# RWKV head groups: the elementwise preparation of the next group is queued beside the block inverse of the current one, behind the scan of the group before; five working buffers get memory of their own

## The reference, cut to what matters

```python
    w = -jax.nn.softplus(-(w0 + jnp.tanh(wl) @ w2)) - 0.5
    a = jax.nn.sigmoid(a0 + al @ a2)
    g = jax.nn.sigmoid(gl) @ g2
    kk = heads(k * k_k)
    kk = kk * lax.rsqrt(jnp.sum(kk * kk, axis=-1, keepdims=True) + 1e-12)
    k = k * (1.0 + (a - 1.0) * k_a)
    decay = jnp.exp(-jnp.exp(heads(w)))

    def step(state, inp):
        r_t, k_t, v_t, kk_t, b_t, d_t = inp
        sa = jnp.einsum('bhvk,bhk->bhv', state, -kk_t)
        state = (state * d_t[:, :, None, :] + sa[..., None] * b_t[:, :, None, :]
                 + v_t[..., None] * k_t[:, :, None, :])
        return state, jnp.einsum('bhvk,bhk->bhv', state, r_t)
...
    y = ((y - mean) * lax.rsqrt(var + LNX_EPS)).reshape(bsz, s, RWKV_W)
    y = y * lnx_g.astype(jnp.float32) + lnx_b.astype(jnp.float32)
    y = y + bonus.reshape(bsz, s, RWKV_W)
    return (y * g.astype(jnp.float32)).astype(feat.dtype)
```

## Time and profile before

| | us |
|---|---|
| median of 3 runs (2466.19 to 2469.96) | 2467.66 |
| time of the profiled execution | 2463.41 |
| its span | 2461.6 |
| PE busy | 2324.6 (94%) |
| DVE busy | 1233.2 (50%) |
| RWKV section, first preparation to last group | 265.6 to 531.0 |

### The profile page before, as it was taken

The page is one execution under the profiler, slowest core; times in us unless marked ns, Lnnn a source line. Parts: engine busy times, 40 slices in busy tenths (PEclk is TensorE's granted clock), DMA queues, the critical chain, the costliest instruction groups (busy, mean ns, idle before and its releaser), DMA issues.

```text
span 2461.6 us, 30787 instructions
## 1 busy us (share of the span) xinstructions
PE 2324.6 (94%) x12524; PEld 1654.6 (67%) x12524; DVE 1233.2 (50%) x2169; ACT 746.1 (30%) x1172; POOL 646.4 (26%) x288
## 2 busy tenths in 40 slices
PE   8989787797999989999999999999999999999999
PEld 3334455544444467668878888888766887888887
DVE  4455555533556531774355767310187445577610
ACT  3333222212111143443233333223354223333311
POOL 0000000002000033224444444444313444444443
PEclk9999888878999999999999999999999999999999
DMA  5521000035999932113333333222211333333322
GB/s 220 135 71 35 15 2 2 2 134 196 373 409 409 356 114 88 60 52 95 94 94 95 98 99 94 93 96 98 86 52 61 94 95 93 96 101 94 95 80 99
DMA packets 80258, 287.79 MB, mean 117 GB/s; under 512 B 9299, under 2 KB 10323, under 8 KB 79478
## 3 DMA queue, kind: packets, MB, share of 16 engines
q1 hardware_dynamic: 76726, 279.56, 33.1%
q0 software_dynamic: 1408, 4.20, 0.5%
q10 hardware_dynamic: 1984, 2.06, 0.2%
HBM read 278.11 MB, written 16.07 MB: 120 GB/s over the span
## 4 chain that ended last, share of the span: by engine, by line
PE 80%; DVE 9%; DMA 5%; issue 3%; ACT 2%; POOL 1%; ACTq 0%; SPq 0%; DVEq 0%; another core or an unknown queue 0%; POOLq 0%
PE bank L1899 12%; PE bank L1901 12%; PE bank L1900 12%; PE bank L529 5%; DMA arena<-in_stream 4%; PE bank L2048 3%; PE bank L2049 3%; PE bank L2047 3%; DVE arena L392 3%; PE bank L1513 2%; PE bank L855 2%; PE bank L1884 2%; PE bank L1886 2%; PE bank L1885 2%; PE bank L1481 2%
## 5 line engine op out<-in xcount | busy, mean ns | idle before, releaser
L1634 POOL TENSOR_TENSOR ring_low<-ring,W_high 128x1024 fp32r<-128x1024 f32 x252 | 606.2, 2406 | 1124.5 <-ACT W_high L402 1124.5
L1899 PE MATMUL bank<-H_high,W_high 128*128 128x512 f32 x1408 | 555.5, 395 | 7.9 <-ACT arena L402 5.9
L1901 PE MATMUL bank<-H_high,ring_low 128*128 128x512 f32 x1408 | 548.5, 390 | 0.0
L1900 PE MATMUL bank<-H_low,W_high 128*128 128x512 f32 x1408 | 548.1, 389 | 0.0
L402 ACT ACTIVATE W_high<-ring 128x1024 fp32r<-128x1024 f32 x264 | 279.8, 1060 | 872.2 <-PE bank L1901 552.6
L1899 PEld LDWEIGHTS bank<-H_high,W_high 128*128 128x128 f32 x1408 | 264.3, 188 | 77.9 <-issue 23.2
L1901 PEld LDWEIGHTS bank<-H_high,ring_low 128*128 128x128 f32 x1408 | 264.3, 188 | 55.9
L1900 PEld LDWEIGHTS bank<-H_low,W_high 128*128 128x128 f32 x1408 | 264.4, 188 | 55.7 <-issue 1.9
L392 DVE TENSOR_TENSOR arena<-bank,root 128x512 f32<-128x512 f32 x116 | 79.7, 688 | 309.9 <-PE bank L1901 309.7
L402 ACT ACTIVATE arena<-bank 128x512 f32<-128x512 f32 (+5 forms) x175 | 74.6, 438 | 315.2 <-PE bank L830 115.9
L398 DVE SCALAR_TENSOR_TENSOR arena<-arena 128x512 f32<-128x512 f32 (+3 forms) x63 | 117.8, 1870 | 99.1 <-ACT arena L406 98.5
(11 more groups left out here) (264 smaller groups left out, 3239.2 us busy)
## 6 DMA issues: line engine op xcount, KB each, us to landing
ring<-in_stream SPq DMA_DIRECT2D x289, 512.0 KB, 3.6
arena<-in_stream SPq DMA_DIRECT2D x31, 2048.0 KB, 12.9
arena<-in_stream SPq DMA_DIRECT2D x31, 1024.0 KB, 10.2
sorted_x<-in_zero_row SPq DMA_DIRECT2D x4, 2048.0 KB
arena<-sorted_x SPq DMA_DIRECT2D x15, 512.0 KB, 16.3
X<-in_x SPq DMA_DIRECT2D x2, 1024.0 KB, 7.9
ring<-in_stream SPq DMA_DIRECT2D x1, 2048.0 KB, 7.9
out<-X SPq DMA_DIRECT2D x8, 256.0 KB, 7.0
```

What stands on the lines that cost most here:

```text
L1634: return G.tensor_tensor(ring_low[:, slot, :], ring[:, slot, :], W_high[:, s % 2, :].bitcast(F32), ALU.subtract)
L1899: mm(ps[:, :], wh[:, k, :], H_high[:, k, :], start=k == 0, stop=False)
L1900: mm(ps[:, :], wh[:, k, :], H_low[:, k, :], start=False, stop=False)
L1901: i = mm(ps[:, :], wl[:, k, :], H_high[:, k, :], start=False, stop=k == KD - 1)
```

## The change: what it does

The generator has three streams now. `rwkv_early` holds the elementwise preparation, cut into `feed` (ru, ra, the two tanh), `rows` (DVE only), `roots` (rkk and ACT's exponentials), `root` (DVE only), `bonus` and `turned`. `rwkv_invert` holds blocks, keyed, the levels and read. `rwkv_scan` is as it was. In round c the inverse of group c, the scan of group c-1 and the early part of group c+1 are dealt out: "i", "s" and "e". Round 0 has no scan and round 3 no early part. The scan of group 3 stands alone at the end, as before. Step and state stand next to each other, between two parts of the inverse.

The product rg and the transpose of v, with their two ACT copies, move from the start of the preparation to its end. The halves get places of their own: half 0 after `feed` of group 0, half 1 after its `roots`, half 2 after its `bonus`, 3 and 4 after `feed` and `bonus` of group 1, 5 after `bonus` of group 2, 6 and 7 after `feed` and `bonus` of group 3. DVE's addition stands at the same place in DVE's queue. Before, there were two halves in each group.

Five buffers of the inverse (MT, TT, TKA, XX, MK) shared memory with buffers of the preparation (LW, A, KK, SQ, RS). They lie in `early` now, over uq, uk and uv, and DVE's wait for `read` of the group before falls away.

```diff
-def rwkv_prepare(c):
-
-    for part in ("rows", "root", "bonus", "turned", "blocks", "keyed"):
-        yield part, c, 0
+def rwkv_invert(c):
+
+    yield "blocks", c, 0
+    yield "keyed", c, 0
     for lev in LEVELS:
         yield "cross", c, lev
         yield "grow", c, lev
...
-BESIDE = "pss" * 4 + "ps" * 10 + "pspp"
+def rwkv_early(c):
+
+    for part in ("feed", "rows", "roots", "root", "bonus", "turned"):
+        yield part, c, 0
+
+
+HALVES_AT = {("feed", 0): [0], ("roots", 0): [1], ("bonus", 0): [2], ("feed", 1): [3], ("bonus", 1): [4], ("bonus", 2): [5], ("feed", 3): [6], ("bonus", 3): [7]}
+BESIDE = "iss" * 4 + "e" + "iss" + "e" + "iss" * 2 + "e" + "iss" + "is" + "e" + "is" * 2 + "e" + "ii" + "e"
...
 def rwkv_order():
 
-    yield from rwkv_prepare(0)
-    for c in range(3):
-        prepare, scan = rwkv_prepare(c + 1), rwkv_scan(c)
+    def with_halves(part):
+        yield part
+        for m in HALVES_AT.get(part[:2], []):
+            yield "half", 0, m
+
+    for part in rwkv_early(0):
+        yield from with_halves(part)
+    for c in range(4):
+        invert, scan, early = rwkv_invert(c), rwkv_scan(c - 1) if c else iter(()), rwkv_early(c + 1) if c < 3 else iter(())
         for who in BESIDE:
-            yield next(prepare if who == "p" else scan)
-        yield from prepare
-        yield from scan
+            part = next({"i": invert, "s": scan}.get(who, early), None)
+            if part is not None:
+                yield from with_halves(part)
+        for rest in (scan, invert, early):
+            assert next(rest, None) is None
     yield from rwkv_scan(3)
...
-    return {"rows": [f"ru{c}", f"ra{c}", f"rg{c}", f"wp{2 * c}", f"rt{c}_v"], "root": [f"rkk{c}"], "bonus": [f"rb{c}", f"wp{2 * c + 1}"],
-            "turned": [f"rt{c}_{x}" for x in "bka"], "blocks": [f"m{x}{c}_{hh}" for x in PRODUCTS for hh in range(2)],
+    return {"feed": [f"ru{c}", f"ra{c}"], "rows": [], "roots": [f"rkk{c}"], "root": [], "bonus": [f"rb{c}"], "half": [f"wp{n}"],
+            "turned": [f"rt{c}_{x}" for x in "bkav"] + [f"rg{c}"], "blocks": [f"m{x}{c}_{hh}" for x in PRODUCTS for hh in range(2)],
...
-        W.update(YB=W["LW"], MT=W["LW"], TT=W["A"], TKA=W["KK"], KH=W["KK"], KT=W["KP"], BT=W["B"], XX=W["SQ"], MK=W["RS"],
+        W.update(YB=W["LW"], KH=W["KK"], KT=W["KP"], BT=W["B"],
                  BH=W["ENL"], AT=W["ELX"])
+        for i, n in enumerate(("MT", "TT", "TKA", "XX", "MK")):
+            W[n] = par(w1, W1, "uq", 512 * i, 512)
...
-            if part == "rows":
+            if part == "half":
+                latent_half(pe, n, range(4))
+            elif part == "feed":
...
+            elif part == "roots":
+                pe.e.wait_ge(*pe.emptied(f"rkk{c}"))
+                pe.e.wait_ge(*pe.nth("kksq", c + 1))
...
+            elif part == "bonus":
+                pe.e.wait_ge(*pe.emptied(f"rb{c}"))
+                pe.e.wait_ge(*pe.nth("rkr", c + 1))
...
+            elif part == "turned":
+                pe.e.wait_ge(*pe.nth("hats", c + 1))
+                for x, src in (("b", W["BH"]), ("k", W["KH"]), ("a", W["AT"]), ("v", RAW[:, 8 + c, 1:513])):
+                    turn_feature(pe, c, x, src)
                 pe.e.wait_ge(*pe.emptied(f"rg{c}"))
...
                 mm(bank_of(f"rg{c}")[:, :], par(w1, W1, "g2", c * P, P), RAW[:, 13, 1:513], start=True, stop=True).then_inc(pe.fills(f"rg{c}"), 1)
-                latent_half(pe, 2 * c, range(0, 2))
-                turn_feature(pe, c, "v", RAW[:, 8 + c, 1:513])
-            elif part == "root":
-                pe.e.wait_ge(*pe.emptied(f"rkk{c}"))
-                pe.e.wait_ge(*pe.nth("kksq", c + 1))
-                mm(bank_of(f"rkk{c}")[:, :], cc("blk64"), W["SQ"], start=True, stop=True).then_inc(pe.fills(f"rkk{c}"), 1)
-                latent_half(pe, 2 * c, range(2, 4))
...
-                latent_half(pe, 2 * c + 1, range(4))
-            elif part == "turned":
-                pe.e.wait_ge(*pe.nth("hats", c + 1))
-                for x, src in (("b", W["BH"]), ("k", W["KH"]), ("a", W["AT"])):
...
-            if part == "rows":
+            if part == "feed":
...
-                sc.e.wait_ge(*sc.filled(f"rg{c}"))
-                if c >= 2:
-                    sc.e.wait_ge(*sc.nth("rw_out", c - 1))
-                act_(W[f"G{q}"], bank_of(f"rg{c}")[:, :], ACT.Copy).then_inc(sc.takes(f"rg{c}"), 1)
-                sc.e.wait_ge(*sc.filled(f"rt{c}_v"))
-                act_(W[f"TKV{q}"], bank_of(f"rt{c}_v")[:, :], ACT.Copy).then_inc(sc.takes(f"rt{c}_v"), 1)
-            elif part == "root":
+            elif part == "roots":
                 log_exp_tables()
...
             elif part == "turned":
-                for x, d in (("b", f"TKB{q}"), ("k", f"TKK{q}"), ("a", "TKA")):
+                for x, d in (("b", f"TKB{q}"), ("k", f"TKK{q}"), ("a", "TKA"), ("v", f"TKV{q}")):
                     sc.e.wait_ge(*sc.filled(f"rt{c}_{x}"))
                     act_(W[d], bank_of(f"rt{c}_{x}")[:, :], ACT.Copy).then_inc(sc.takes(f"rt{c}_{x}"), 1)
+                sc.e.wait_ge(*sc.filled(f"rg{c}"))
+                if c >= 2:
+                    sc.e.wait_ge(*sc.nth("rw_out", c - 1))
+                act_(W[f"G{q}"], bank_of(f"rg{c}")[:, :], ACT.Copy).then_inc(sc.takes(f"rg{c}"), 1)
...
-            if part == "rows":
-                if c:
-                    dv.e.wait_ge(*dv.filled(f"rta{c - 1}_1"))
+            if part == "half":
+                add_latent_half(dv, n)
+            elif part == "feed":
                 ts(w["KK"], k_, one("k_k"), None, ALU.mult).then_inc(dv.tells("kk0"), 1)
+            elif part == "rows":
...
                 tt(c64(w["KH"]), c64(w["KT"]), dc, ALU.mult).then_inc(dv.tells("hats"), 1)
                 V.tensor_copy(w[f"DC{q}"], c64(w["EL"])[:, :, 63]).then_inc(dv.chained(), 1)
-                add_latent_half(dv, 2 * c)
             elif part == "bonus":
                 dv.e.wait_ge(*dv.filled(f"rb{c}"))
                 tt(w[f"BON{q}"], bank_of(f"rb{c}")[:, :], v_, ALU.mult).then_inc(dv.takes(f"rb{c}"), 1)
-                add_latent_half(dv, 2 * c + 1)
```

More of the change, by code:

```diff
@@ L458, in build @@
             W[f"DC{q}"] = arena[:, 27968 + 8 * q:27976 + 8 * q]
-        W.update(YB=W["LW"], MT=W["LW"], TT=W["A"], TKA=W["KK"], KH=W["KK"], KT=W["KP"], BT=W["B"], XX=W["SQ"], MK=W["RS"],
+        W.update(YB=W["LW"], KH=W["KK"], KT=W["KP"], BT=W["B"],
                  BH=W["ENL"], AT=W["ELX"])
+        for i, n in enumerate(("MT", "TT", "TKA", "XX", "MK")):
+            W[n] = par(w1, W1, "uq", 512 * i, 512)
+        assert [W1[n] for n in ("uq", "uk", "uv")] == [(0, 1536), (1536, 512), (2048, 512)]
         halves_ = [slice(0, 64), slice(64, 128)]
@@ L719, in rwkv_pe @@
                 mm(bank_of(f"ra{c}")[:, :], w2a2[64:128, cw], RAW[64:128, 12, 1:513], start=True, stop=True).then_inc(pe.fills(f"ra{c}"), 1)
+            elif part == "roots":
+                pe.e.wait_ge(*pe.emptied(f"rkk{c}"))
+                pe.e.wait_ge(*pe.nth("kksq", c + 1))
+                mm(bank_of(f"rkk{c}")[:, :], cc("blk64"), W["SQ"], start=True, stop=True).then_inc(pe.fills(f"rkk{c}"), 1)
+            elif part == "bonus":
+                pe.e.wait_ge(*pe.emptied(f"rb{c}"))
+                pe.e.wait_ge(*pe.nth("rkr", c + 1))
+                mm(bank_of(f"rb{c}")[:, :], cc("blk64"), W["YB"], start=True, stop=True).then_inc(pe.fills(f"rb{c}"), 1)
+            elif part == "turned":
+                pe.e.wait_ge(*pe.nth("hats", c + 1))
+                for x, src in (("b", W["BH"]), ("k", W["KH"]), ("a", W["AT"]), ("v", RAW[:, 8 + c, 1:513])):
+                    turn_feature(pe, c, x, src)
                 pe.e.wait_ge(*pe.emptied(f"rg{c}"))
@@ L723, in rwkv_pe @@
                 mm(bank_of(f"rg{c}")[:, :], par(w1, W1, "g2", c * P, P), RAW[:, 13, 1:513], start=True, stop=True).then_inc(pe.fills(f"rg{c}"), 1)
-                latent_half(pe, 2 * c, range(0, 2))
-                turn_feature(pe, c, "v", RAW[:, 8 + c, 1:513])
-            elif part == "root":
-                pe.e.wait_ge(*pe.emptied(f"rkk{c}"))
-                pe.e.wait_ge(*pe.nth("kksq", c + 1))
-                mm(bank_of(f"rkk{c}")[:, :], cc("blk64"), W["SQ"], start=True, stop=True).then_inc(pe.fills(f"rkk{c}"), 1)
-                latent_half(pe, 2 * c, range(2, 4))
-            elif part == "bonus":
-                pe.e.wait_ge(*pe.emptied(f"rb{c}"))
-                pe.e.wait_ge(*pe.nth("rkr", c + 1))
-                mm(bank_of(f"rb{c}")[:, :], cc("blk64"), W["YB"], start=True, stop=True).then_inc(pe.fills(f"rb{c}"), 1)
-                latent_half(pe, 2 * c + 1, range(4))
-            elif part == "turned":
-                pe.e.wait_ge(*pe.nth("hats", c + 1))
-                for x, src in (("b", W["BH"]), ("k", W["KH"]), ("a", W["AT"])):
-                    turn_feature(pe, c, x, src)
             elif part == "blocks":
```

## The result

| | before | after |
|---|---|---|
| median of 14 runs, us | 2466.09 (2464.17 to 2469.96) | 2472.68 (2467.72 to 2473.92, and one of 2976) |
| profiled execution, its span | 2463.41, 2461.6 | 2473.22, 2471.4 |

The ratio is 1.0022 (95%: 1.0015 to 1.0029): the change makes the kernel 6.6 us slower, where the prediction had 10.9 us faster.

What follows compares the result with a forecast made beforehand. The prediction saw neither PE nor DVE full: elementwise preparation and the inverse's chain make PE wait, and its clock drops. A walk of -19.9 us plus 9 for the clock gave -10.9, so 2456.8 us, range 2445 to 2470.5.

Steps and rivals of the forecast that it cites:

- the clock term: Rounds 0 to 2: slow PE stretches behind waits for DVE cost 9 us, bounds 0 and 20.
- I count six of these: Rounds 0 to 2: two PE waits for DVE each, 3.3 to 4.3 us long, with a slow stretch behind each.
- I take 3.4: Microseconds PE works at the lower clock behind each such wait, read from the first gap of the kernel before.
- I take 9: Clock loss: 8.4 us for six slow stretches, and perhaps one more thin place between `turned` and the blocks.
- walk: PE's and DVE's queues in the RWKV section followed round by round at full clock: sum -19.9 us.
- Stage A: Early part of group 0, 16.9 us before: +1.5 us, bounds -1.4 and +5.
- Rounds 0 to 3 of the walk: Lengths 45.8, 54.8 and 58.4 us for rounds 0 to 2; changes of +18.7, -9.0, -6.1 and -25.0 over rounds 0 to 3.
- buffers: New places in memory of the five buffers: costed at nothing, since shapes and types are as before.
- Case 2: Rival: step and state overlap level products better (7 us), or the clock holds (4 us); gain 17 to 25 us, chance 0.24.
- Case 3: Rival: preparation only changes its place, `rows` and `root` hold up the inverse; -5 to +5 us, chance 0.18.
- Case 4: Rival: halves behind `root` or ahead of `rows` run at the low clock; +4.5, up to +12 us, chance 0.07.
- Case 5: Rival: short pauses make the clock oscillate through rounds 0 to 2; +25, so +5 us over before, chance 0.03.

Runs made afterwards that it cites:

- x2_fill: The changed kernel with 33 unread products on PE where it waits for DVE: median 2441.65 us, 0.9906 of the kernel before.
- y4: The changed kernel with unread products only at the rounds' start (two ahead of step 0, one ahead of state 0): 2456.84 us, 0.9950 of before.
- x1: The kernel before with the five buffers moved and nothing else: 2465.96 us, 1.0004 of before.
- z3: The kernel before with unread products: four ahead of state 0, eight ahead of step 1, two ahead of step 4: 2458.37 us, 0.9967 of before.
- x3_rotate: The changed kernel with a round beginning with one scan step in place of step, state and step, the rest shifted along: 2465.24 us, 1.0000 of before.
- z1: The changed kernel with halves 2 to 7 behind `rows` and `root` and unread products where waits were left: 2428.16 us, 0.9857 of before.
- x4: The changed kernel with all halves but 1 placed where PE waits for `rows` or `root`: 2444.48 us, 0.9918 of before.
- y1: The kernel before with unread products, four ahead of state 0 and five ahead of step 1 of each round: 2466.54 us, 1.0005 of before.

## Why the prediction was wrong

**The step that failed is the clock term** ("I count six of these", "I take 3.4", "I take 9. Bounds: 0 [...] and 20"). The rounds, from the first block product to the next one (round 3 to step 0 of the last scan), show this. x2_fill stands for full clock.

| | walk | x2_fill | after | after - x2_fill |
|---|---|---|---|---|
| round 0 | 45.8 | 45.1 | 49.8 | 4.7 |
| round 1 | 54.8 | 53.3 | 64.6 | 11.3 |
| round 2 | 58.4 | 56.9 | 68.3 | 11.4 |
| round 3 | 40.3 | 38.5 | 43.8 | 5.3 |

With 1.5 us outside the rounds this makes 34.2 us (538.13 - 503.92). Some 1 us of it isn't the clock's: the two traces were that far apart at the first products of group 0 (262.87 and 261.82), ahead of all fillers. Against the kernel before, x2's section ends 27.7 us earlier, where the walk had 19.9; it was 7.8 us too cautious. So -19.9 - 7.8 + 34.2 = +6.5. This sum closes by the way in which its two new terms are taken, both from x2. What stands by itself is the count of slow work below.

The term was off in all of its factors:

- *How many.* I counted the waits of over 3 us. The pair of 1.73 and 1.11 us at each round's start was in my own walk (masks hold DVE for 6.3 us, step 0 behind them), but I costed it as time only. y4 prices it at some 14 us. Round 3 had one of these at its start too (0.83), where I counted none.
- *How long.* I took 3.4 us from one row of before, as the shortest reading of it. In the three stretches of round 1 PE worked for 12.4, 8.1 and 5.6 us at the lower level.
- *How much is lost.* I took the 1.20 us of the earlier trace rows as a time at the lower level. It isn't one: the clock rose within it (0.67 over 478 to 480 in the kernel before). The same 58 level products in the changed kernel, at 0.50 and at 1.00, give a share of 1 - 1.85/3.34 = 0.45 lost, in place of 0.37:

```profile
348.36 3.34 PE L871 MATMUL bank<-early 64*64 64x64 f32 x58
...
357.28 1.85 PE L871 MATMUL bank<-early 64*64 64x64 f32 x58
```

The time that PE worked at the lower level, added up from windows of 0.1 us, is 11.1, 26.2, 26.2 and 12.7 us in rounds 0 to 3 of the changed kernel and none in x2_fill. At 0.45 that costs 5.0, 11.8, 11.8 and 5.7 us. The differences measured in the table are 4.7, 11.3, 11.4 and 5.3. So the slow work accounts for each round's loss.

**Stage A**: +0.8 (17.7 against 16.9) for +1.5. The number is right, in part by luck: PE worked at the lower level for 6.6 us of it before and for 1.1 after, which the prediction didn't have. **Rounds 0 to 3 of the walk** were right, each 0.7 to 1.8 us too long at full clock. The waits came where they were put and at their length. x1 bears out the **buffers**.

**The rivals.** Case 2 (the overlap is better) has the size right, 7.8 us for its 7, but its place in part only: 4.8 of them lie in the three rounds with a scan, the others in round 0, in stage A and at the end. That the 4.8 come from overlap wasn't tested. Case 3 has its number of -5 to +5 just missed. Its reason (`rows` and `root` hold up the inverse as they did the start of the round) is wrong by x2 and z3; its condition, slow stretches that eat the walk's gain, is what happened, with 34 us for its 14 to 20. Case 4, halves at low clock, is a small part: the halves behind `root` took 4.23, 4.49 and 4.48 us for 3.6, the others in the rounds 3.70. The one in round 1 (PE's timeline):

```profile
387.80 4.49 PE L528 MATMUL bank<-H,ring 128*128 128x512 f32 x8
```

Its way to "slower" was nearest in kind, but it looked at the wrong products: what ran slow were level products and scan steps. Case 5, an oscillation in every short pause, didn't come: in round 0 of x2_fill PE is busy for 39.55 of 45.1 us, with the pauses between level products as they were, and the clock is 1.00. The Trainium skill's section "A second HAM failure mode: psum-queue depth-cycling" in "TensorE: Matmul & The Clock Gate" says that short idle times between groups of products made the clock of one kernel go back and forth between its levels. At the round's start this case goes that way (waits of 1.73 and 1.11 us, then 0.60 and 0.50 of the clock), and round 0's inverse in x2_fill stands against it.

**What a better term would have been,** in hindsight. The second wait of before had PE working at the lower level from 327.79 to 336, for 8.2 us; I took the first, with 3.4. With 8.2 us, 0.45 lost and nine places (six counted and three round starts) the term is 33 us, near the 34 measured, and outside my own upper bound of 20. The sum would have been +13, which has the way right and is off by the 7.8 us of the walk. The kernel before doesn't lose this much itself: PE worked at the lower level for 38.5 us in its three rounds, 17 us at 0.45, but z3 won back only 9. One reason can be read in the earlier trace rows: the first stretch (318.9 to 322.3) is followed by a wait of 4.86 us for DVE, in which its slowness mostly hides. In the new order the slow stretches lie on the path.

**What stays open.** Why the clock came back after 3.4 us of work in x3_rotate and after 12.4 in the changed kernel, with PE recorded as busy for 2.00 of 2 us in both, isn't settled. Two things differ: x3 has one short wait where the changed kernel has two, and other products follow (what stands first in the round differs by a state and a step). No run parts these. Nor is it settled which short waits lower the clock. A wait of 1.73 us at the same place of round 0 (ahead of `keyed`, 288.02) left it at 1.00 in the changed kernel, one of 1.63 us (347.33) did so in the kernel before, and in z1's round 0 two of 0.7 us, with six products between them, were followed by the lower level. The division of x4's gain is an estimate and not a measurement.

## What to carry to other kernels

When a change moves the waits of PE, work out the sum at full clock first and then ask at which places PE will stand empty, short ones too, and what stands behind each: here a good order (17 to 18 us at equal clock) lost some 33 us to that. What counts is the time that PE then works at the lower level on the path, here at 0.45 lost. Put work that is needed anyway into those waits (x4: 28 us with the same instructions); unread products may fill the rest (z1: 38 us under the kernel before). Fill a wait to its end, for fillers that stop early can bring nothing: in y1 the slow stretches came behind what was left of the waits, and no time was gained.

## What the runs showed of the hardware

- Two waits of 1.73 and 1.11 us, with 0.64 us of products between them, were followed by 12.4 us of work at the lower of the two clock levels (1.2 GHz), although PE was recorded as busy for 13.39 of 14 us there.
- The slow stretches weren't of one length: 3.4, 5.6, 8.1 and 12.4 us of work in round 1 of two kernels. In the last scan of the changed kernel and up to the section's end, 24 of PE's 25.6 us of work ran at the lower level, though PE was recorded as busy for 1.96 to 2.00 of 2 us in each window from 512 to 526.
- The same 58 level products took 3.34 us at the lower level and 1.85 at full clock.
- 33 unread products, some 30 us of PE's time by a half's row, made a launch 31 us shorter (2472.68 to 2441.65).
